# Forgetting attention in units of two heads that lie in the two partition halves

## The reference, cut to what matters

```
def _fox_attention(q, k, v, c):
    # logit[t,s] = q_t.k_s/sqrt(d) + c_t - c_s, per-frame causal
...
        s = jnp.einsum('bhqd,bhkd->bhqk', qb, k) * scale + (cb[..., :, None] - c[..., None, :])
        mask = k_pos[None, :] <= q_pos[:, None]
        p = jax.nn.softmax(jnp.where(mask, s, MASK_VALUE), axis=-1)
        return jnp.einsum('bhqk,bhkd->bhqd', p, v)
...
def _odd_mixer(x, w_in, w_out, b_f, qn_g, kn_g):
    q, k, v, g, f_logit = jnp.split(x @ w_in, ...)          # 16 heads of 64
    qh, kh = _rms_norm(heads(q), qn_g), _rms_norm(heads(k), kn_g)
    c = jnp.cumsum(jax.nn.log_sigmoid(f_logit + b_f), axis=1)
    o = _fox_attention(qh, kh, vh, c)
    return (o * jax.nn.sigmoid(g)) @ w_out
```

## Time and profile before

| | us |
|---|---|
| median of three runs | 1485.17 (1483.53 to 1485.54) |
| the profiled execution | 1485.66 |
| its span in the profile | 1483.9 |
| PE busy | 1398.3 |
| ACT busy | 499.9 |
| DVE busy | 480.5 |
| POOL busy | 527.6 |

### The profile page before, as it was taken

One profiled execution on the slowest core, in us unless ns is written; L12 is line 12 of the kernel. 1 busy time (PEld: TensorE's weight loads), 2 busy tenths in 40 slices (PEclk: granted clock), 3 DMA queues, 4 the chain that ended last, 5 costly groups with the idle time before them and its releaser, 6 DMA issues.

```text
span 1483.9 us, 19200 instructions
## 1 busy us (share of the span) xinstructions
PE 1398.3 (94%) x7244; PEld 1174.8 (79%) x7244; DVE 480.5 (32%) x1120; ACT 499.9 (34%) x824; POOL 527.6 (36%) x421
## 2 busy tenths in 40 slices
PE   7999996799999999999899998889899999999997
PEld 6888874578888888887778887877679888888886
DVE  3366526553111111014536271533362111110005
ACT  4313236424223232112435554544323222323120
POOL 5421312044544445351342222202134454454450
PEclk9999998899999999999999999979799999999999
DMA  6311121022333233322232121012012323324231
GB/s 220 112 32 57 58 86 57 1 86 70 101 105 94 86 99 111 102 85 59 86 114 58 58 58 57 1 64 80 29 57 86 113 86 96 104 71 140 73 114 57
DMA packets 136891, 119.53 MB, mean 81 GB/s; under 512 B 5472, under 2 KB 112096, under 8 KB 136800
## 3 DMA queue, kind: packets, MB, share of 16 engines
q1 hardware_dynamic: 136800, 118.31, 25.6%
HBM read 116.20 MB, written 2.10 MB: 80 GB/s over the span
## 4 chain that ended last, share of the span: by engine, by line
PE 81%; DVE 8%; ACT 6%; issue 3%; POOL 1%; DMA 0%; ACTq 0%; DVEq 0%; POOLq 0%; SPq 0%
PE banks L445 24%; PE banks L447 24%; PE banks L446 24%; PE banks L856 2%; PE banks L874 2%; ACT w_hi L980 1%; PE banks L720 1%; PE banks L516 1%; PE banks L865 1%; ACT p_fox L1202 1%; POOL w_lo L940 1%; DVE small L1534 1%; DVE xT_lo L1254 1%; PE banks L820 1%; PE banks L787 1%
## 5 line engine op out<-in xcount | busy, mean ns | idle before, releaser
L940 POOL TENSOR_TENSOR w_lo<-w_raw,w_hi 128x512 fp32r<-128x512 f32 x417 | 527.3, 1297 | 920.2 <-ACT w_hi L980 920.2
L445 PE MATMUL banks<-xT_lo,w_hi 128*128 128x512 f32 (+2 forms) x928 | 344.9, 372 | 2.8 <-DVEq L1256 2.8
L447 PE MATMUL banks<-xT_hi,w_hi 128*128 128x512 f32 (+2 forms) x928 | 343.1, 370 | 0.0
L446 PE MATMUL banks<-xT_hi,w_lo 128*128 128x512 f32 (+2 forms) x928 | 342.9, 370 | 0.0
L980 ACT ACTIVATE w_hi<-w_raw 128x2048 fp32r<-128x2048 f32 (+1 forms) x107 | 200.0, 1869 | 201.3 <-PE banks L447 167.0
L445 PE MATMUL banks<-w_lo,xT_hi 128*128 128x512 f32 (+1 forms) x608 | 222.6, 366 | 11.4 <-ACT o_fox L1002 3.9
L447 PE MATMUL banks<-w_hi,xT_hi 128*128 128x512 f32 (+1 forms) x608 | 215.2, 354 | 0.0
L446 PE MATMUL banks<-w_hi,xT_lo 128*128 128x512 f32 (+1 forms) x608 | 214.7, 353 | 0.0
L445 PEld LDWEIGHTS banks<-xT_lo,w_hi 128*128 128x128 f32 (+1 forms) x928 | 173.9, 187 | 32.6 <-issue 3.5
L447 PEld LDWEIGHTS banks<-xT_hi,w_hi 128*128 128x128 f32 (+1 forms) x928 | 173.7, 187 | 29.7
L446 PEld LDWEIGHTS banks<-xT_hi,w_lo 128*128 128x128 f32 (+1 forms) x928 | 173.9, 187 | 29.5
(11 more groups left out here) (165 smaller groups left out, 1271.9 us busy)
## 6 DMA issues: line engine op xcount, KB each, us to landing
w_raw<-in_ffn_w_dram SPq DMA_DIRECT2D x92, 512.0 KB, 3.9
w_raw<-in_ffn_w_dram SPq DMA_DIRECT2D x20, 1024.0 KB, 5.0
w_raw<-in_fox_w_in_dram SPq DMA_DIRECT2D x16, 1024.0 KB, 5.8
w_raw<-in_even_w_in_dram SPq DMA_DIRECT2D x14, 1024.0 KB, 5.0
w_raw<-in_even_w_out_dram SPq DMA_DIRECT2D x4, 1024.0 KB, 5.1
w_raw<-in_fox_w_out_dram SPq DMA_DIRECT2D x4, 1024.0 KB, 6.4
x_res<-in_x_dram SPq DMA_DIRECT2D x4, 512.0 KB, 8.0
out_dram<-x_res SPq DMA_DIRECT2D x4, 512.0 KB, 2.6
```

Source lines behind the costliest of these rows:

```text
L445: mm(acc, l_hi, r_lo, start=first, stop=False)
L446: mm(acc, l_lo, r_hi, start=False, stop=False)
L447: return mm(acc, l_hi, r_hi, start=False, stop=final)
L940: ins = nc.gpsimd.tensor_tensor(w_lo[c % RING][:, a:a + n], w_raw[c % RAW][:, a:a + n], w_hi[c % RING][:, a:a + n].bitcast(F32), ALU.subtract)
```

## The change

A unit is now two heads, `pair`, and one block: 32 units, and 35 steps of the pipeline in place of 67. q and k are kept two heads to a tile, in partitions 0 to 63 and 64 to 127 (`qk`), without the two additional columns; a piece needs two transposes. The two heads' scores are two products of 64 rows into two banks. The term `-c_s` is added by a bf16 product of three rows, the three bf16 pieces of `-c`, against ones (L868); `c_t` is left out, since the softmax doesn't see it. The pieces come by twelve small transfers (`c_rows`) that SP issues before the chunk `foxq1`. The banks are dealt anew: two for pieces, one for heads and for the first head's transposes, one for the second's, three for scores, one for values. The maximum is taken for both heads (one operation or two), the probabilities are divided by their sum before the transpose (`fnorm`), and the values product is turned round: `v_all` is stationary, 64 columns of it, the transposed probabilities move, 128 columns, and the two heads write the two partition halves of one bank. So the output comes out feature-major (`oT`), the gate is computed feature-major (as tanh, which shares a table with the exponential), and the 32 transposes at the end are gone; ACT and DVE split `oT` by `out_hi` and `out_lo`. All 64 pieces remain: 16 in the lead, and 12 in each quarter of the units; the last two units have none, but PE does there, and in the two steps behind, the first chunk of the output projection.

```diff
+FOX_LEAD = [("q", 0), ("k", 0), ("v", 0)]
+FOX_PARTS = [[("q", 1), ("k", 1), ("v", 2)], [("q", 2), ("k", 2), ("v", 3)], [("q", 3), ("k", 3), ("g", 0)],
+             [("g", 1), ("g", 2), ("g", 3)]]
...
+            share = [[2, 1] * 4, [2, 1] * 4, [2] * 4 + [1] * 4, [2] * 6 + [0] * 2][j]
...
+        SCORE_BANKS = [(5, 6), (5, 7), (6, 7)]
...
+                for m, acc in enumerate(accs):
+                    rows = slice(m * HD, (m + 1) * HD)
+                    mm(acc[:, 0:n], qk[rows, j % 2, 0, pair % 2, i * P:(i + 1) * P], qk[rows, j % 2, 1, pair % 2, 0:n],
+                       start=True, stop=False)
+                for m, acc in enumerate(accs):
+                    h = 2 * pair + m
+                    rows = slice(32 * (h % 4), 32 * (h % 4) + 3)
+                    mm(acc[:, 0:n], ones_bf[rows, 0:1].to_broadcast([3, P]), c_rows[rows, h // 4, 0:n],
+                       start=False, stop=False)
...
+                for j in range(i + 1):
+                    for m in range(2):
+                        h = 2 * pair + m
+                        ins = mm(psum[2][m * HD:(m + 1) * HD, tok], v_all[:, j, h * HD:(h + 1) * HD],
+                                 pT_fox[:, u % 2, m, j * P:(j + 1) * P], start=j == 0, stop=j == i)
...
                 if heads_at(i - 1):
                     part, j, t, n = heads_at(i - 1)
-                    acc = full((f"fox{'qk'[part]}{j}", t))
+                    key = (f"fox{'qk'[part]}{j}", t)
                     if n >= 2:
-                        act.wait_ge(S["qvar"], n - 1)
-                    chain(fn(sq[:, n % 2, :], acc[:, 0:256], ACT.Square), S["sq_done"])
+                        act.wait_ge(S["qn_done"], n - 1)
+                    evac(key, q_raw[:, n % 2, :], lambda acc: acc[:, 0:256])
+                    chain(fn(sq[:, n % 2, :], q_raw[:, n % 2, :], ACT.Square), S["sq_done"])
...
+                if s is not None and 1 <= s <= F_UNITS:
+
+                    u = s - 1
+                    n, c = (u % NT + 1) * P, 2 * (u % 4)
+                    dve.wait_ge(S["fexp"], u + 1)
+                    step(v.reciprocal(small[:, 32 + c:34 + c], small[:, 24 + c:26 + c]))
+                    for m in range(2):
+                        p = p_fox[:, u % 3, m, 0:n]
+                        ins = ts(p, p, small[:, 32 + c + m:33 + c + m], None, ALU.mult)
+                        chain(ins, S["fnorm"] if m else dve_step)
```

More of the change, by code:

```diff
@@ L159, in build @@
         small = place("small", [48], F32, 4)
+        ones_bf = place("ones_bf", [2], BF16, 2)
         top[0] = -(-top[0] // 128) * 128
@@ L580, in tile @@
                     tok = slice(t * P, (t + 1) * P)
-                    for n, (c, k0) in enumerate(parts):
+                    for n, (c, src_hi, src_lo, k0) in enumerate(parts):
                         if t == 0:
@@ L834, in _ @@
+            first_out[1] = token_chunk(chunk_at("out1"), "dve", o_hi4, o_lo4, 0, True, False, places=(0, 1, 6, 7))
+            for i, (piece, s) in enumerate(fox_steps):
                 if piece and i >= 2:
@@ L1157, in _, with out_hi, prob_copy @@
             swiglu_act(0)
-            def fox_gates(half):
-                for t in range(NT):
-                    evac((f"foxg{half}", t), fox_gate(half, t), whole, ACT.Sigmoid)
-                    act.sem_inc(S["g_done"], 1)
-            for i, (piece, s) in enumerate(fox_slots):
+            def out_hi(f, tok=slice(0, TS), n=0):
+                act.wait_ge(S["o_gated"], f + n + 1)
+                dst = o_hi4[:, f, tok] if f < 4 else xT_hi[:, f, tok]
+                chain(fn(dst, oT[:, f, tok], ACT.Copy, scale=0.5), S["o_hi"])
+            def prob_copy(u):
+                n = (u % NT + 1) * P
+                acc = full(("fT", u, 0))
+                if u >= 2:
+                    full(("fv", u - 2))
+                release(fn(pT_fox[:, u % 2, 0, 0:n], acc[:, 0:n], ACT.Copy), ("fT", u, 0))
+                act.sem_inc(S["fpT_a"], 1)
+            for i, (piece, s) in enumerate(fox_steps):
                 if i == 0:
@@ L1497, in fox_heads @@
             def fox_heads(part, j, t, n):
-                key = (f"fox{'qk'[part]}{j}", t)
                 m = fox_ms[:, n % 2, :, :]
@@ L1553, in _ @@
+                f = gate_at(i - 1)
+                if f is not None and f <= 5:
+                    chain(out_gate(f, oT[:, f, :]), S["o_gated"])
+                if f == 2:
+                    out_lo(0)
+                if f is not None and 2 <= f <= 4:
+                    out_lo(f - 1)
             mixer_tail(1)
```

427 lines of the change are left out of this document (247 added, 180 removed).

## The result

| | us |
|---|---|
| before, beside it on the same chip | 1485.36 (1483.53 to 1488.04, 4 runs) |
| the changed kernel | 1444.56 (1443.57 to 1448.37, 4 runs) |
| ratio | 0.9734, 95% interval 0.9716 to 0.9752 |
| span of its profiled execution | 1441.4 (before 1483.9) |

What follows compares the result with a forecast made beforehand. PE was taken to bound the kernel, by its own work plus waits and half clock. Gains of -47.8 us and additions of 10, 2 and 4 gave -31.8: 1485.7 to 1454 us, range 1434 to 1475.

Steps and rivals of the forecast that it cites:

- (i): Lead before the first unit: ACT and DVE do more while PE, on two banks, can't run ahead; +4 us, bounds 0 and 10.
- (f): Stalls in the middle: the gate needs no table and each unit has pieces beside it; -6 and -13 us.
- (g): DVE, slowed beside POOL, at or over PE's pace in some 16 of 32 units; +10 us, bounds 0 and +30.
- (h): Pieces have two banks, so some piece a chunk waits for ACT's copy behind its 1.9 us rounding; +2 us.
- (a): Scores on PE: a pair of heads falls from 4.80 to 3.40 us, a gain of 11.2 us for eight.
- (b): New forget-term products on PE: 0.9 + 4 x 0.1 us a pair, 10 us in all.
- (c): Values product turned round: a key block of two heads from 0.42 to 0.34 us; -6.4 us, bounds -16 and +2.
- (d): Turning a q or k piece: two transposes (0.22 us) in place of four (0.43), 32 pieces; -7 us.
- (e): End, last mask to output projection: 19.8 us become 5.4, projection pieces covering the last chain; -14.4 us.
- One of the signs that the prediction names for being wrong: Wrong if the clock falls in q/k stretches, L897 costs over 0.44 a key block, or the lead grows over 10 us.
- Rival 1: Whole kernel PE-bound after all: DVE's lag is absorbed and the values' column halves overlap; 1433 us, chance 0.2.
- Rivals 2 to 4: DVE and ACT set the pace, 1468 to 1483 (0.17); no measurable change (0.04); slower, every unit stalling, 1508 (0.05).

Runs made afterwards that it cites:

- The head-by-head run: Changed kernel with all value products of one head first, then all of the other, in place of alternating by key block: ratio 0.9779, layer +7.1 us.
- the late projection: Changed kernel with the output projection's first chunk begun after the attention, not dealt between its last four steps: ratio 0.9786, layer +8.2 us.
- Order and lock: Two edits to the changed kernel: ACT copies turned heads before its root (0.9653); POOL makes low parts of only 512 columns a chunk (0.9668); both 0.9610.
- the kernel that copies first: Changed kernel with ACT copying the turned heads out of their bank before the square root that waits for DVE's variance: 1434.51 us, ratio 0.9653.

## Why the prediction was right, and where its terms were off

The sign, the mechanisms of the gain and the range were right; the time came out 9 us below the forecast. The terms furthest off are the lead (i), by 4.8 us, and the stalls (f, g, h together), by 3.1. Terms of both signs were mis-sized and partly cancel, so it is in part luck that the sum is only 9 us off.

- **(a), (b)** together -3.0 us (8 pairs of heads, 4.80 to 4.42), forecast -1. The forget term costs 0.96 a pair, 7.7 in all, forecast 10. The two heads' products of three rows run side by side: 0.16 to 0.32 us in four steps is 0.053 for each further 128 columns of both heads, no more than one mask of 128 columns took in the earlier trace rows (0.06).
- **(c)** -8.3 us, forecast -6.4. A pair's four blocks take 2.78 us. Before they took 3.8, not the 4.20 that (c) starts from: 0.42 a key block was read from a unit with four, and with fewer a key block costs less (timeline of PE of the kernel before, one and two key blocks of a head):

```profile
790.95 0.33 PE L874 MATMUL banks<-v_all,pT_fox 128*128 128x64 f32 x2
791.09 0.36 PE L445 MATMUL banks<-w_lo,xT_hi 128*128 128x256 f32 x1
...
795.42 0.56 PE L874 MATMUL banks<-v_all,pT_fox 128*128 128x64 f32 x4
795.78 0.36 PE L445 MATMUL banks<-w_lo,xT_hi 128*128 128x256 f32 x1
```

  One to four key blocks of a head took 0.14, 0.36, 0.59 and 0.81 us, 1.90 together and 3.8 for two heads. The step that failed is "nearer the serial end because the products are short". The column halves overlap wholly: a further key block of both heads costs 0.22 us, where two heads paid 0.45. What keeps the gain small is 0.15 fixed a block and the smaller sum to begin with. The Trainium skill (TensorEngine Tiling (Array Packing), Overview, with the swap itself under Performance Considerations) promises up to twice the speed: the trace agrees for a further key block, 0.45 to 0.22, but the -16 that the prediction worked out by it didn't come. The head-by-head run shows that the gain hangs on the order: 6 of the 8 us go when more than four records of one half stand in a row.
- **The transposes of probabilities** have no term in the sum ("stay 160"). They cost 2.9 us more: 0.32, 0.54, 0.77 and 0.97 us for one to four key blocks of two heads, where two heads took 0.23, 0.45, 0.66 and 0.89. Why isn't shown; they are now dealt over two banks.
- **(d)** -3.8 us (0.43 to 0.31, 32 pieces), forecast -7. Half the transposes don't halve the time; about 0.1 us doesn't scale.
- **(e)** -13.4 us, forecast -14.4. Shown by the late projection: without the pieces between, 6.7 of it is lost again. The term also charges all 5.4 us of attention behind the last mask to the end, though the kernel before had some 2.9 there (at the full clock) and the rest only moved there from between the units: 2.2 us that the sum loses. The 6 us that the forecast put on a failed cover were a fair price for the waits (4.6); the cold clock was missing in it.
- **(f)** "Both places are units without, or with few, pieces beside them" was right as a description, but the cure wasn't mainly the spread: with four bare units in a row only 2.7 us of layer return. What remains is the unit itself, two heads with a lag of two, which I didn't separate further. All 28 us of idle time and cold clock between first scores and last mask were replaced, where 19 were counted.
- **(g), (h)** What came in their place is 17.9 us there (14.8 idle, 3.1 clock), forecast 12. So f, g and h together are -10, forecast -7. One of the signs that the prediction names for being wrong did show: the clock fell in these stretches, to 0.97 in two quarters. The step "DVE is at or over PE's pace in some 16 of 32 units" failed: in the three quarters DVE was busy 61% (115.7 of 188.5 us; the forecast's 11.9 of 14 is 85%). Nor did PE wait for `fnorm`, and at the scores only once, 1.1 us; it waited for a copy on ACT whose place in the program stands behind DVE's variance. "ACT, which waits for the variance before it goes on to the exponential, falls back with it" was the right sentence about the wrong victim: what stood behind the root first was not the exponential but the copy of the heads, on which bank 3 hangs. Order and lock are worth 11.4 and 6.7 us of layer; with both mended the three quarters went from 188.5 to 174.5, 14 of the 17.9 us. The lock itself is as described: 6.7 us of layer, the four-element operation at 1.16 us. The Trainium skill (VectorE: DVE Perf Modes, Two Vector instructions with no wait between them) has the shared interface; with POOL's work cut to a quarter none of 24 was stretched, and the trace agrees.
- **(h)** Outside the lead PE waited 2.8 us for `q_raw`, forecast 2.
- **(i)** -0.8 us in place of +4. The step "while PE, on two banks, can't run ahead" took the banks for the harm. With four banks PE ran ahead, and the lead got 4.5 us longer.
- **Rival 1** (PE-bound, overlap, 1433) was half true: the overlap came, the stalls stayed; the kernel that copies first lands there, at 1434.5. Rivals 2 to 4 rested on DVE's list as the pace and fell with it.

Summed from the first piece to the second chunk of the output projection, with (a) to (d) and the transposes as -3.0 - 8.3 - 3.8 + 2.9 = -12.2: -12.2 of work, -2.2 of work that moved from between the units to behind the last mask, where (e) carries it, -13.4 of the end, -1.2 for the first pieces of the projection at the lower clock, -10.1 of stalls and clock, -0.8 of the lead. That is -39.9 against the -41 measured between the marks, and -39.5 by the ratio (0.0266 of 1485). The 1 us between sum and marks is open.

## What to carry to other kernels

When a rearrangement shares a buffer between two uses, look at what stands ahead of the operation that frees it, in the program of the engine that does it: an in-order engine that first waits for a late partner holds the buffer for all that time, and swapping two blocks of its program was worth 11 us here, while two more banks in the lead cost 4.5. Count an engine's load for its pace, but look for the late link by following one wait back through three engines. And put long work that has to be done anyway between the last, thin steps of a pipeline: here it hid 4.6 us of waits and kept the granted clock at 1.00 in place of 0.56.

## What the runs showed of the hardware

- Two column halves of the array ran side by side on f32 products of 128 columns at full overlap (0.22 us for four records), when the halves alternate; with four records of one half in a row it cost 0.01 to 0.05 us a unit. With six or eight in a row the surplus ran alone: 0.27 and 0.49 us more.
- A product of 64 moving columns was no quicker than one of 128: a further key block of one head, two records, cost 0.22 us with 64 columns of values, and a further 128 keys of the scores, two records as well, 0.215.
- In all these shapes 0.1 to 0.15 us did not scale: two transposes 0.31, values 0.15 + 0.22 a key block, the forget term 0.11 + 0.053 for each 128 columns of both heads.
- A DVE operation of four elements a partition (0.17 us) that began beside one of POOL's took until that one was over, 1.16 to 1.22 us, in six of 24 cases; with three quarters of POOL's operations gone it happened in none.
- Giving PE two more banks, and so room to run ahead, made the lead longer: 12.6 us of waits in place of 8.0, with the same work on ACT and DVE.
